# A Fourier stage on half of its channel frequencies, with the norm applied behind the first transform

## The reference

```python
def rms_norm(x, g):
    y = x32 * lax.rsqrt(jnp.mean(x32 * x32, axis=-1, keepdims=True) + EPS)
    return (y * g.astype(jnp.float32)).astype(x.dtype)

def fourier_mix(h, w_f):
    b, n, d = h.shape
    hg = h.astype(jnp.float32).reshape(b, n, N_FOURIER_GROUPS, FOURIER_GROUP)   # 4 groups of 256
    f = jnp.fft.fft2(hg, axes=(1, 3), norm="ortho").real
    return f.reshape(b, n, d).astype(h.dtype) @ w_f

# layer 1, x only
x = x + 0.5 * mx[2] * swiglu(modulate(rms_norm(x, norm_g[1, 0]), mx[0], mx[1]), ffn1...)
hx = modulate(rms_norm(x, norm_g[1, 1]), mx[3], mx[4])      # h * (1 + scale) + shift
x = x + mx[5] * fourier_mix(hx, fourier_w[0])
x = x + 0.5 * mx[8] * swiglu(...)
```

## Time and profile before

| | |
|---|---|
| median of three runs | 1992.72 us (1989.61 to 1995.20) |
| the profiled execution | 1993.38 us, span 1991.6 us |
| PE busy | 1910.8 us (96% of the span), 12107 instructions |
| VectorE / ScalarE busy | 1425.9 us (72%) / 1004.8 us (50%) |
| chain that ended last, by engine | PE 88%, VectorE 6%, ScalarE 2% |
| HBM read | 380.57 MB, 192 GB/s over the span |
| mean granted TensorE clock | 0.981 of full speed |

### The profile page before, as it was taken

One profiled execution on the slowest core, in us unless ns is written; L12 is line 12 of the kernel. 1 busy time (PEld: TensorE's weight loads), 2 busy tenths in 40 slices (PEclk: granted clock), 3 DMA queues, 4 the chain that ended last, 5 costly groups with the idle time before them and its releaser, 6 DMA issues.

```text
span 1991.6 us, 31675 instructions
## 1 busy us (share of the span) xinstructions
PE 1910.8 (96%) x12107; PEld 1659.4 (83%) x12107; DVE 1425.9 (72%) x2027; ACT 1004.8 (50%) x1526; POOL 0.2 (0%) x4
## 2 busy tenths in 40 slices
PE   4999999999999999999998999999999989999997
PEld 3777777766776899999996999999988978878776
DVE  5789999974847676677665566676866664578886
ACT  3325675643325454455445454455445454467775
POOL 0000000000000000000000000000000000000000
PEclk8999999999989999999999999999999989999999
DMA  9757987983301366667564266665544365679995
GB/s 328 227 176 236 302 277 230 299 271 101 101 22 43 106 178 182 181 184 201 173 179 139 86 192 176 181 181 164 164 131 137 102 222 170 191 251 361 333 336 186
DMA packets 516365, 383.33 MB, mean 192 GB/s; under 512 B 13817, under 2 KB 473978, under 8 KB 515986
## 3 DMA queue, kind: packets, MB, share of 16 engines
q1 hardware_dynamic: 515728, 381.36, 62.5%
q10 hardware_dynamic: 514, 0.30, 0.1%
HBM read 380.57 MB, written 1.05 MB: 192 GB/s over the span
## 4 chain that ended last, share of the span: by engine, by line
PE 88%; DVE 6%; ACT 2%; SPq 1%; DMA 1%; issue 1%; DVEq 0%; ACTq 0%
PE ps L2258 17%; PE ps L2260 17%; PE ps L2259 17%; PE ps L2890 4%; PE ps L2892 4%; PE ps L2891 4%; PE ps L2271 2%; PE ps L2272 2%; PE ps L2273 2%; PE ps L2908 2%; PE ps L2906 2%; PE ps L2907 2%; DVE lo L1372 1%; ACT hi L869 1%; SPq L648 1%
## 5 line engine op out<-in xcount | busy, mean ns | idle before, releaser
L2258 PE MATMUL ps<-nhi,hi 128*128 128x258 f32 (+2 forms) x1920 | 590.3, 307 | 0.0
L2260 PE MATMUL ps<-nhi,lo 128*128 128x258 f32 (+2 forms) x1920 | 587.9, 306 | 0.0
L2259 PE MATMUL ps<-nlo,hi 128*128 128x258 f32 (+2 forms) x1920 | 586.0, 305 | 0.0
L1372 DVE TENSOR_TENSOR lo<-raw,hi 128x1024 fp32r<-128x1024 f32 (+2 forms) x388 | 460.4, 1189 | 116.5 <-ACT hi L869 116.2
L869 ACT ACTIVATE hi<-raw 128x1024 fp32r<-128x1024 f32 (+2 forms) x388 | 395.3, 1023 | 249.2 <-PE ps L2260 189.7
L2258 PEld LDWEIGHTS ps<-nhi,hi 128*128 128x128 f32 x1920 | 364.4, 190 | 34.0 <-issue 16.6
L2260 PEld LDWEIGHTS ps<-nhi,lo 128*128 128x128 f32 x1920 | 363.7, 189 | 16.8
L2259 PEld LDWEIGHTS ps<-nlo,hi 128*128 128x128 f32 x1920 | 363.5, 189 | 16.2
L2258 PE MATMUL ps<-hhi,hi 128*128 128x256 f32 (+1 forms) x576 | 177.3, 308 | 0.0
L2259 PE MATMUL ps<-hlo,hi 128*128 128x256 f32 (+1 forms) x576 | 176.6, 307 | 0.0
L2260 PE MATMUL ps<-hhi,lo 128*128 128x256 f32 (+1 forms) x576 | 176.6, 307 | 0.0
(11 more groups left out here) (383 smaller groups left out, 3157.5 us busy)
## 6 DMA issues: line engine op xcount, KB each, us to landing
raw<-in_ffn_w_gu SPq DMA_DIRECT2D x176, 512.0 KB, 4.7
modw<-in_w_mod SPq DMA_DIRECT2D x56, 1024.0 KB, 7.1
raw<-in_ffn_w_d SPq DMA_DIRECT2D x64, 512.0 KB, 4.4
raw<-in_w_in SPq DMA_DIRECT2D x36, 512.0 KB, 4.0
raw<-in_w_exp_gate SPq DMA_DIRECT2D x36, 512.0 KB, 5.0
raw_more<-in_w_exp_up SPq DMA_DIRECT2D x36, 512.0 KB, 5.3
mod_early<-in_w_mod SPq DMA_DIRECT2D x16, 1024.0 KB, 10.5
raw<-in_w_exp_down SPq DMA_DIRECT2D x32, 512.0 KB, 5.5
```

The source lines that it names most:

```text
L1372: v.tensor_tensor(lo[:, s], raw[:, s], hi[:, s].bitcast(F32), ALU.subtract).then_inc(lo_ready, 1)
L2258: pe.matmul(bank(u, T), w_hi(u, k), h_, start=(k == 0), stop=False)
L2259: pe.matmul(bank(u, T), w_hi(u, k), l_, start=False, stop=False)
L2260: ins = pe.matmul(bank(u, T), w_lo(u, k), h_, start=False, stop=(k == nk - 1))
```

## The change

It rests on the symmetry of the reference. Per group only 128 frequency columns (1 to 127 and, in the last place, 0) are computed, as cosine and sine; the chunk for 255 down to 129 is the same data with its tokens read in reverse order. In the last place of that chunk stands frequency 128, whose row is made apart (`edges`) and put at partition 127 by a DMA. The rows of `fourier_w` are put in this order on the host, ahead of the launch. The shift enters as two columns: it is the same for all tokens, so it touches token frequency 0 alone.

Gain is applied to `xs` in l1f1.down2 by ScalarE (`late_hi`); the reciprocal norm is one number per token, and after the first transform tokens lie on partitions, so it becomes a scale of the copies to `yt`: `rstd` is 128x2. Squares are summed by `token_sums` with `sqsum` as the stationary operand and one column of ones.

```diff
+SPEC_W = 2 * P + 2
+N_DFT = 2 * SPEC_W + 4 * SPEC_W                 # columns of dft: 1548, before 2048
+SPEC_BANK = ((5, 6), (7, 4), (0, 1), (2, 3))
+FREQ_BANK = (5, 6, 7, 4)
+EDGE_BANK = 3
 # SyncE
             plain("fourier", t["fourier_w"][0], 0)
+            sp.wait_ge(S["y_copied"], FOURIER_GROUPS + 2)
+            for dst, src in ((hhi, edge_hi), (hlo, edge_lo)):
+                sp.dma_start(edge_rows(dst).bitcast(F32), src[:, :].bitcast(F32)).then_inc(S["in_dft"], 16)
             ffn("l1f2", t["ffn2_w_gu"][1], t["ffn2_w_d"][1])
 # ScalarE
+                if s == FOURIER_NORM:      # in late_hi(late, k)
+                    nc.scalar.activation(xf[:, k * SEQ:(k + 1) * SEQ], chunk(xs, k, part=X_COLS), ACT.Copy, scale=gain(k)).then_inc(S["xf_ready"], 1)
+                    return
-            ffn("l1f1", SEQ, squares=(4, SEQ))
-            norm(4, SEQ, mod_shift((2,), 1), full=xf)
-            for i in range(8):
-                act.wait_ge(S["y_done"], i + 1)
-                nc.scalar.activation(yt[:, 512 * i:512 * i + 512], bank(i % 4), ACT.Copy).then_inc(S["y_copied"], 1)
-            for c in range(KD):
-                act.wait_ge(S["f_done"], c + 1)
-                nc.scalar.activation(chunk(hhi, c, part=X_COLS), bank(4 + c % 4, SEQ), ACT.Copy).then_inc(S["f_hi"], 1)
+            ffn("l1f1", SEQ, squares=(4, SEQ), late=mod_late(FOURIER_NORM, 2, 1))
+            norm_root(FOURIER_NORM, 2)
+            act.wait_ge(rstd_ready, FOURIER_NORM + 1)
+            for g in range(FOURIER_GROUPS):
+                act.wait_ge(S["y_done"], 2 * g + 1)
+                nc.scalar.activation(spectrum(g, 0), bank(SPEC_BANK[g][0], SPEC_W), ACT.Copy, scale=rstd[:, 0:1]).then_inc(S["y_copied"], 1)
+            def freq_hi(g, n):
+                act.wait_ge(S["f_done"], n)
+                nc.scalar.activation(frequencies(hhi, g), bank(FREQ_BANK[g], SEQ + 1), ACT.Copy).then_inc(S["f_hi"], 1)
+                act.wait_ge(S["f_hi"], 2 * g + 1)
+                nc.scalar.activation(chunk(hhi, FOURIER_GROUPS + g, part=X_COLS)[0:P - 1], turned_tokens(hhi, g), ACT.Copy).then_inc(S["f_hi"], 1)
+            # freq_hi(0, 1), freq_hi(1, 2), then edge_hi (4x256) from bank 3, then freq_hi(2, 4), freq_hi(3, 5)
 # VectorE
+            v.tensor_scalar(shift16[...], modc[...], 16.0, None, ALU.mult)       # 128x16, ahead of l1f1
-            norm(4, SEQ, mod_gain((2,), 1), mod_shift((2,), 1), split=False)
-            late_split("l1f1.down2")
-            for c in range(KD):
-                dve.wait_ge(S["f_hi"], c + 1)
-                v.tensor_tensor(chunk(hlo, c, part=X_COLS), bank(4 + c % 4, SEQ), chunk(hhi, c, part=X_COLS).bitcast(F32), ALU.subtract).then_inc(S["f_lo"], 1)
+            norm_var(FOURIER_NORM, 2, bank(4, 2, 510))
+            dve.wait_ge(rstd_ready, FOURIER_NORM + 1)
+            for g in range(FOURIER_GROUPS):
+                dve.wait_ge(S["y_done"], 2 * g + 2)
+                v.tensor_scalar(spectrum(g, 1), bank(SPEC_BANK[g][1], SPEC_W), rstd[:, 1:2], None, ALU.mult).then_inc(S["f_lo"], 1)
+                if g == 1:
+                    late_split("l1f1.down2")
+            # freq_lo(0), freq_lo(1), edge_lo (4x256), freq_lo(2), freq_lo(3): a subtraction and a turned copy each
 # TensorE
-            ffn("l1f1", SEQ, 3, squares=(4, SEQ))
-            pe.wait_ge(evacuated, U * ph["fourier"][0])
+            ffn("l1f1", SEQ, 3)
+            def over_width(g):             # two token halves, two matmuls of 258 columns each
+                pe.wait_ge(S["xf_ready"], 2 * g + 2)
+                ...
+            def token_sums():              # four matmuls of one column
+                ...
+            def over_tokens(g):
+                pe.wait_ge(S["y_copied"], g + 1)
+                pe.wait_ge(S["f_lo"], g + 1)
+                o = bank(FREQ_BANK[g], SPEC_W)
+                for tc in range(2):
+                    for sine in range(2):
+                        pe.matmul(o, spectrum(g, tc)[:, sine * P:(sine + 1) * P], token_waves(tc, sine, SPEC_W), start=(tc == sine == 0), stop=False)
+                for k in range(2):
+                    c = 2 * g + k
+                    ins = pe.matmul(o[:, 0:SEQ + 1:SEQ], dft[:, SPEC_W * k:SPEC_W * k + P], shift16[:, 2 * c:2 * c + 2], start=False, stop=(k == 1))
+                ins.then_inc(S["f_done"], 1)
+            def edges():                   # y_copied, f_lo >= 4; two matmuls of 256 columns, two of one
+                ...
+            pe.wait_ge(S["in_dft"], 16)
+            pe.wait_ge(evacuated, U * ph["fourier"][0] - 2)
+            over_width(0)
+            over_width(1)
+            token_sums()
+            over_width(2)
+            pe.wait_ge(evacuated, U * ph["fourier"][0])
+            over_width(3)
+            over_tokens(0)
+            over_tokens(1)
+            edges()
+            over_tokens(2)
+            over_tokens(3)
             def f_chunk(k):
-                if k + 4 < KD:
-                    over_tokens(k + 4)
-                pe.wait_ge(S["f_lo"], k + 1)
+                if k == FOURIER_GROUPS:
+                    pe.wait_ge(S["in_dft"], 48)
+                g, turned = k % FOURIER_GROUPS, k // FOURIER_GROUPS
+                pe.wait_ge(S["f_hi"], 2 * g + 1 + turned)
+                pe.wait_ge(S["f_lo"], FOURIER_GROUPS + 2 * g + 1 + turned)
```

More of the change, by code:

```diff
@@ L49 @@
 LATE_ROWS = 7
+FOURIER_GROUPS = 4
+FREQ = tuple(range(1, P)) + (0,)
+SPEC_W = 2 * P + 2
+N_DFT = 2 * SPEC_W + 4 * SPEC_W
 N_EXPERTS = 16
@@ L183, in make_constants, with fourier_rows @@
     }
+def fourier_rows():
+    rows = [256 * g + k for g in range(FOURIER_GROUPS) for k in FREQ]
+    return rows + [256 * g + 256 - (k or P) for g in range(FOURIER_GROUPS) for k in FREQ]
 def phases():
@@ L335, in build @@
         A.at = modw_at
-        dft = A("dft", 2048)
+        dft = A("dft", N_DFT)
         xf = A("xf", KD * SEQ)
-        yt = A("yt", 2 * 4 * 512)
+        yt = A("yt", 2 * FOURIER_GROUPS * SPEC_W)
+        shift16 = A("shift16", 2 * KD)
+        edge_hi = A("edge_hi", SEQ, F32R, parts=FOURIER_GROUPS)
+        edge_lo = A("edge_lo", SEQ, F32R, parts=FOURIER_GROUPS)
         A = At(region)
@@ L997, in norm_root, with norm_hi @@
                 nc.scalar.activation(rstd[:, 0:T], rv_[:, 0:T], ACT.Sqrt).then_inc(rstd_ready, 1)
-            def norm_hi(s, T, shift, full=None, between=None):
+            def norm_hi(s, T, shift, between=None):
                 for k in range(KD):
@@ L1581, in gates_of, with norm_var, norm_apply @@
                 return lambda c: [gcol[:, bass.ds(24 * k + 8 * s + c, 1)] for k in sets]
-            def norm_var(s, T):
+            def norm_var(s, T, sums=None):
                 dve.wait_ge(sq_summed, s + 1)
-                v.tensor_scalar(rs[:, 0:T], bank(4, T), 1.0 / D, EPS, ALU.mult, ALU.add).then_inc(var_ready, 1)
+                v.tensor_scalar(rs[:, 0:T], bank(4, T) if sums is None else sums, 1.0 / D, EPS, ALU.mult, ALU.add).then_inc(var_ready, 1)
                 dve.wait_ge(var_ready, 2 * s + 1)
                 v.reciprocal(rv_[:, 0:T], rs[:, 0:T]).then_inc(var_ready, 1)
-            def norm_apply(s, T, gain, shift, split=True):
+            def norm_apply(s, T, gain, shift):
                 dve.wait_ge(rstd_ready, s + 1)
@@ L1602, in norm_apply @@
                 for k in range(KD):
-                    if k >= 2 and split:
+                    if k >= 2:
                         dve.wait_ge(nlo_ready, splits_before(s) + k - 1)
-                    elif k >= 2:
-                        dve.wait_ge(S["xf_ready"], k - 1)
                     for a, at in zip(gain(k), (T - SEQ, 0)):
@@ L1611, in norm_apply @@
                     ins.then_inc(nt_ready, 1)
-                    if k and split:
+                    if k:
                         lo_of(k - 1)
-                if split:
-                    lo_of(KD - 1)
+                lo_of(KD - 1)
             def mod_late(s, c, part):
@@ L2691, in _ @@
                         at = (2 * g + k) * SEQ + tc * P
-                        ins = pe.matmul(bank(i % 4), xf[:, at:at + P], dft[:, 512 * k:512 * k + 512], start=(k == 0), stop=(k == 1))
+                        ins = pe.matmul(bank(SPEC_BANK[g][tc], SPEC_W), xf[:, at:at + P], dft[:, SPEC_W * k:SPEC_W * (k + 1)], start=(k == 0), stop=(k == 1))
                     ins.then_inc(S["y_done"], 1)
[L2695 to L2703, removed]
-                ins.then_inc(S["f_done"], 1)
@@ L2706, in _ @@
-            for c in range(4):
-                over_tokens(c)
-            def f_chunk(k):
-                if k == 0:
-                    pe.wait_ge(S["y_copied"], KD)
-                if k + 4 < KD:
-                    over_tokens(k + 4)
-                pe.wait_ge(S["f_lo"], k + 1)
+            def token_sums():
+                pe.wait_ge(sq_ready, KD * (FOURIER_NORM + 1))
+                pe.wait_ge(sq_used, (KD - 1) * (FOURIER_NORM + 1))
+                for tc in range(2):
```

(25 more changed lines are left out.)

60 lines of the change are left out of this document (39 added, 21 removed).

## The result

The changed kernel takes **1969.14 us** (median of 4 runs, 1967.37 to 1970.72), against 1991.16 (1988.42 to 1995.20) for the kernel before on the same chip, now with one run more than the table above has. The ratio is 0.9888, with a 95% interval of 0.9866 to 0.9909: 22.0 us less, between 18.1 and 26.7. The forecast was 20.2 less, and a time of 1973. The profiled execution took 1968.14 us, with a span of 1966.3.

What follows compares the result with a forecast made beforehand. TensorE, busy 96% of the span, was taken as the bound. The stage's 19.3 us plus 0.9 for `dft` gave 20.2 off the profiled 1993.38, 1973.2, forecast as 1973; bounds 1970 to 1976, with rivals 1 and 4 1969 to 1979.

Steps and rivals of the forecast that it cites:

- The stage: Fourier stage, from l1f1.down2's end to the first slab behind the pair: 23.54 us against 42.82, 19.3 less.
- first transform: Start of the Fourier stage: 16 matmuls, 32 passes at 0.218 us, 6.96 in place of 16.14.
- second transform: Fourier stage, behind `token_sums`: 16 matmuls, 32 passes at 0.218 us, 6.96; shift matmuls priced separately.
- shift: Within the second transform: eight two-column matmuls, 16 passes at 0.115 us, 1.84.
- the pair: End of the Fourier stage: 48 fp32r matmuls at 0.115 us each, 5.54, unchanged.
- the five-column row: Twenty five-column passes in the earlier profile, 2.29 us, at full clock: taken as price of a thin pass, 0.115 us.
- What waits: Fourier stage: squares, norm, scaled copies, hi/lo splits and edge rows all ready in time; TensorE waits 0, edge rows at most 1.5 us.
- The second gain: Ahead of l1f1's first weights on SyncE's queue: `dft` load 256 KB smaller, 0.9 us less, between 0 and 2.0.
- rival 1: Fourier stage: 28 short or gapped passes cost 0.259 us each, not 0.115; 4.0 us more, time 1977; chance 0.07.
- rival 4: Behind the stage, or at the first transform's start: some 5 us given back, time 1978; chance 0.05.
- rival 2: Fourier stage: all at 1.2 GHz costs about 19 us, time 1992, no change; chance 0.03.
- rival 3: The pair's chunk 4 waits for edge-row DMAs landing over 26 us behind issue: slower, time from 1999; chance 0.02.

Runs made afterwards that it cites:

- Experiment 9: Changed kernel with `token_sums` moved behind the whole first transform, from between `over_width(1)` and `over_width(2)`: 1970.85 us in one execution, stage 26.49.
- experiment 5: Changed kernel with the `dft` load padded with zeros back to 2048 columns (1024 KB): 1966.26 us in one execution.
- experiment 6: Changed kernel with the `dft` load issued behind l1f1's first weights instead of ahead of them: 1968.73 us (4 runs), ratio 0.990.
- experiment 7: Changed kernel with the wait for both edge-row DMAs moved from the pair's chunk 4 to chunk 0: 1972.03 us in one execution.
- experiment 8: Changed kernel with the two-column shift matmuls writing adjacent PSUM columns 0 and 1 instead of 0 and 256: 1968.11 us in one execution, stage 23.46.
- experiment 1: The kernel before, run and profiled once more with no edit: 1984.02 us; ten other runs beside it had a median of 1991.35.
- after's repeat: The changed kernel, run and profiled once more with no edit: 1972.68 us, stage 23.40.
- experiment 3: Changed kernel's half of the frequencies, but the norm in front of the first transform as in the kernel before: 1976.64 us, ratio 0.9921, stage 28.97.
- experiment 10: Changed kernel with the eight shift matmuls of `over_tokens` left out: 1969.08 us in one execution, stage 21.72.
- experiment 4: Changed kernel's late norm, but all frequencies and both transforms as in the kernel before, shift as one column: 1984.32 us (7 runs), ratio 0.9967, stage 37.69.

## What the prediction had right, and the step that failed

**The stage: right, 23.45 against a forecast of 23.54.** By its terms:

| term | forecast | measured |
|---|---|---|
| first transform, 32 passes | 6.96 | 3.49 + 3.60 = 7.09 |
| `token_sums`, 8 passes | 0.92 | 0.12 + 3 x 0.22 = 0.79 with rounding |
| second transform, 32 long passes | 6.96 | 7.38 |
| shift, 16 thin passes | 1.84 | 4 x 0.34 = 1.36 |
| `edges` | 1.32 | 1.04 |
| the pair | 5.54 | 5.80 |

A thin pass takes 0.085 us in the shift, less than the 0.115 taken from the five-column row; a long pass behind thin ones starts about 0.1 late, a cost that the prediction put at nothing. The pair's matmuls are 0.118 us apart, not 0.115. The thin terms came out 0.9 too dear and the long ones 0.8 too cheap: they cancel, and that 23.54 and 23.45 are so close is in part luck. The prediction's own range for the thin pass reached down to 0.05, so 0.085 lies in it.

**What waits: right.** The order held with margins close to those worked out: `rstd` 0.62 behind `token_sums` (forecast 0.9), the last scaled copy 3.75 ahead of `edges` (3.7), the turned copies no dearer than straight ones (0.42 on ScalarE, where the nearest rows were 0.4 to 0.5), ScalarE's eight new pieces without a wait of TensorE. Experiment 9 shows that the margin was worth something: with none of it the cost is 3.0 us.

**The second gain: right in kind.** 0.9 was forecast; the two profiles give 0.95, with a wait of 1.17 where "near 1.2" was said. All traces together give about 0.6, and the padded load did not land squarely on either side, so its size stays open; that the load stands in the weights' way there is shown by moving it (17.25).

**The total: the step that failed is the base and its scatter.** The time is 3.9 us below the forecast of 1973 and 0.9 below the lowest of the forecast's own bounds, 1970 to 1976. It lies in the wide range, 1969 to 1979, by 0.14 us, and that is luck: this range is wide for rivals 1 and 4, which lie above the forecast and didn't come true, and its lower edge has no working. The bounds add up what `dft`, the thin passes, the edge rows and ScalarE could do, and hold the kernel before at its median of three runs; for how far that moves they have no term. The sentence that ought to have been one is "before, single runs lay 3 us to either side of the median". The runs show more in its place: medians of the same kernel of 1991.16 (4 runs), 1991.35 (10) and 1988.80 (7, beside experiments 5 to 8), and one execution at 1984.02, 7.3 under the median beside it.

Of the 3.9 us, 1.6 is the base: 1992.72 from three runs became 1991.16 with the fourth. 0.5 is how the forecast was rounded from 1972.5. The last 1.8 is the difference of the two kernels, 22.0 against 20.2, and with an interval of 18.1 to 26.7 it can't be told from nothing. No trace gives it a place in the change either: stage and `dft` interval together give 20.3 in the first pair of profiles and 18.8 in the second. Where it comes from stays open.

What scatters is shown in part. It is work that the change doesn't touch, and mostly a matter of how long the lower clock lasts in it: attention (experiment 1), and a stretch behind the stage, here in the first profile before and in the first after, at the same place of the work, with one wait of 2.8 us in both (columns as in the earlier trace rows):

```profile
1350.00:1360.00 10.00, 7.20 (x50) 6.81 (x49) 7.42 (x14) 6.47 (x9) 0.00 (x0) 0.83 0.54 158
1327.00:1337.00 10.00, 7.20 (x62) 6.85 (x62) 7.42 (x14) 6.38 (x9) 0.00 (x0) 1.00 0.53 159
```

So the difference of the two profiles, 25.3, is no measure of the change: 5 us of it lie where nothing was changed, and repeats of both kernels move these parts either way. The prediction had it right that the stage gives 19.3 and that the rest of the work stays; it took the time of that rest as fixed.

**The rivals.**
1. *Short and gapped passes don't overlap*: wrong. They take 0.085, not 0.259, and the gap costs nothing (experiment 8).
2. *The clock falls in the stage*: it didn't (1.00), but it can: in experiment 9 a wait of 1.3 us behind thin passes brought it down, for 1.9 us. The twenty thin passes that kept the clock were the right row to go by: the change's thin passes stand in unbroken work too.
3. *Late edge rows*: wrong, landed within 3.5 us, where it needed 26 (experiment 7).
4. *Given back behind the stage*: wrong, as far as the scatter lets it be seen. The rest behind the stage took 862.76 and 863.80 us after, 865.13 and 864.05 before, and between 862.5 and 865.4 in all twelve traces.

What isn't settled: what sets the pace of l1f1 in an execution, and why the lower clock lasts longer in one attention than in another when the waits are the same. I tried no kernel for either.

## What to carry to other kernels

A linear stage behind a norm needn't wait for it: the per-token factor can be applied to the results, and TensorE then computes through the norm, provided that some microseconds of its own work stand between the sums and the first use (3.6 here; with none it was 1.3 us of wait and 1.9 by the clock). Where the bound engine runs back to back, its instructions counted by shape and multiplied by rows of the same shape give a stage to a few per cent. Weigh such a sum against the same stage of both traces, not against the difference of two executions, which here was 5 us too much for the first pair and 7.5 too little for the repeats. And give the time of the untouched rest a term of its own in the range.

## What was not expected of the hardware

- **Two paces at a full clock.** L1f1 took 172.6 us in some executions (before's repeat, the first after, experiments 5 and 8), 174.2 to 174.5 in six others (the first before, after's repeat, experiments 3, 6, 7 and 10) and 175.6 in experiments 4 and 9. Those last two hold the fall of the clock at l1f1's start that experiment 9 shows, and in the window from 900 to 1050 they have 1250 and 1251 matmuls, so they are the slow pace and not a third. In the windows shown, with PE never idle and 1.00 granted, that is 1265 or 1251 matmuls in the same 150 us, 0.1186 or 0.1199 us each.
- **A short wait can cost more by the clock than by itself.** 1.3 us of idling behind eight one-column passes cost 1.9 us more by the clock, while up to 2.24 us behind long passes, at the start of l1f1, left it at 1.00.
- **Thin passes are cheap in themselves and dear for their neighbour**: 0.085 us for each of two columns, and about 0.1 for the long pass behind a group of them.
- **Reading backwards costs ScalarE nothing that shows**: 0.42 us for 256 turned columns. The straight pieces of the same shape at L997 of the kernel after take 0.40. VectorE's turned copies take 0.29.
